# Attention scores from operands stacked to 128 rows, with the row of maxima passed through DRAM

## The reference

```python
def block(args):
    qn, qr = args
    s = (jnp.einsum('bqhd,bkhd->bhqk', qn, k_nope)
         + jnp.einsum('bqhd,bkd->bhqk', qr, k_rope)).astype(jnp.float32) * scale
    p = jax.nn.softmax(s, axis=-1).astype(v.dtype)
    return jnp.einsum('bhqk,bkhd->bqhd', p, v)
```

## Time and profile before

| | us |
|---|---|
| median of three runs | 3884.38 (3883.72 to 3888.82) |
| profiled execution, its own time | 3887.53 |
| its span, first to last instruction | 3885.8 |
| TensorE busy | 3559.1 (92%) |
| VectorE busy | 2205.4 (57%) |
| ScalarE busy | 1532.3 (39%) |
| GpSimd busy | 218.2 (6%) |

### The profile page before, as it was taken

How to read it: one execution, slowest core, us unless ns; L and a number is a source line. 1 busy time by engine, 2 the same in 40 slices (tenths; PEclk the granted TensorE clock), 3 DMA queues, 4 the chain that set the end, 5 groups by cost and what they waited for, 6 DMA issues and landing times. The chain is left out here.

```text
span 3885.8 us, 51505 instructions
## 1 busy us (share of the span) xinstructions
PE 3559.1 (92%) x19453; PEld 2991.9 (77%) x19453; DVE 2205.4 (57%) x3803; ACT 1532.3 (39%) x1959; POOL 218.2 (6%) x132
## 2 busy tenths in 40 slices
PE   5999969997999999999599739999999999999991
PEld 4888868875777777776477628999999999999991
DVE  4444457766777777776355454555555555545545
ACT  2111134444666666666223213433333333333335
POOL 0000000001000000000011100100000000000100
PEclk9999989998999999999899859999999999999995
DMA  2112145656211222200433124555555555555546
GB/s 105 60 59 74 53 156 202 217 212 140 53 20 39 55 53 53 53 8 5 144 135 135 76 87 142 162 168 169 158 176 157 157 172 163 167 167 157 165 127 241
DMA packets 314712, 470.46 MB, mean 121 GB/s; under 512 B 79073, under 2 KB 215009, under 8 KB 311905
## 3 DMA queue, kind: packets, MB, share of 16 engines
q1 hardware_dynamic: 302816, 426.94, 34.8%
q0 software_dynamic: 11776, 41.95, 5.1%
HBM read 352.83 MB, written 116.00 MB: 121 GB/s over the span
## 5 line engine op out<-in xcount | busy, mean ns | idle before, releaser
L63 PE MATMUL psum<-xeT_hi,w_hi 128*128 128x320 f32 x2048 | 635.2, 310 | 0.0
L64 PE MATMUL psum<-xeT_lo,w_hi 128*128 128x320 f32 x2048 | 633.5, 309 | 0.0
L65 PE MATMUL psum<-xeT_hi,w_lo 128*128 128x320 f32 x2048 | 633.5, 309 | 0.0
L1915 ACT ACTIVATE w_hi<-w_raw 128x2048 fp32r<-128x2048 f32 x192 | 358.6, 1908 | 295.5 <-PE psum L65 199.5
L1993 DVE TENSOR_TENSOR w_lo<-w_raw,w_hi 128x2048 fp32r<-128x2048 f32 x192 | 432.3, 2285 | 40.3 <-ACT w_hi L1915 40.3
L1228 ACT ACTIVATE p_hi<-psum 128x1024 fp32r<-128x1024 f32 x272 | 279.1, 1026 | 360.6 <-PE psum L65 360.6
L1275 DVE TENSOR_REDUCE mx<-psum 128x1 f32<-128x1024 f32 x256 | 312.9, 1224 | 168.9 <-PE psum L1152 168.9
L63 PEld LDWEIGHTS psum<-xeT_hi,w_hi 128*128 128x128 f32 x2048 | 385.1, 188 | 1.0
L64 PEld LDWEIGHTS psum<-xeT_lo,w_hi 128*128 128x128 f32 x2048 | 385.2, 188 | 0.6
L65 PEld LDWEIGHTS psum<-xeT_hi,w_lo 128*128 128x128 f32 x2048 | 385.2, 188 | 0.0
L1293 DVE TENSOR_TENSOR p_lo<-p_raw,p_hi 128x1024 fp32r<-128x1024 f32 x272 | 333.2, 1225 | 82.8 <-ACT p_raw L1230 79.5
(11 more groups left out here) (323 smaller groups left out, 6835.2 us busy)
## 6 DMA issues: line engine op xcount, KB each, us to landing
w_raw<-in_w_gate SPq DMA_DIRECT2D x64, 1024.0 KB, 6.2
w_raw<-in_w_up SPq DMA_DIRECT2D x64, 1024.0 KB, 9.4
w_raw<-in_w_down SPq DMA_DIRECT2D x64, 1024.0 KB, 5.2
rec<-rec SPq DMA_DIRECT2D x20, 768.0 KB, 3.6
recb<-rec SPq DMA_DIRECT2D x20, 768.0 KB, 5.1
xa<-in_x SPq DMA_DIRECT2D x20, 512.0 KB, 4.4
xb<-in_x SPq DMA_DIRECT2D x20, 512.0 KB, 6.0
xo<-in_x SPq DMA_DIRECT2D x20, 512.0 KB, 3.4
```

What stands on the lines that cost most here:

```text
L63: pe.matmul(out, a[0], b[0], start=first, stop=False)
L64: pe.matmul(out, a[0], b[1], start=False, stop=False)
L65: return pe.matmul(out, a[1], b[0], start=False, stop=last)
L1915: a.activation(w_hi[n % 4][:], raw[n % 4][:], ACT.Copy).then_inc(s["hi_made"], 1)
```

## The change

A score is k_hi q_hi + k_lo q_hi + k_hi q_lo over 96 features, less the maximum. The 288 rows of that sum are laid anew, as 128 + 128 + 32, with the maximum as a 33rd row of the last part:

- `k_a`, `q_a`: nope high by nope high (64), rotary high by rotary high (32), rotary high (keys) by rotary low (queries) (32).
- `k_b`, `q_b`: nope low (keys) by high (64), nope high (keys) by low (64).
- `k_c`, `q_c`: rotary low (keys) by rotary high (32) and the maxima (keys' row -1, queries' row the maximum). The first key tile of a slot has these on partitions 0 to 32, the second on 64 to 96, so `k_c` has half as many columns, and `q_c` holds its rows twice.

A slot's scores are four matmuls of 128 rows and then two of 33 rows. A head's load is then ten transfers of q and k rows (512 rows of 10 KB instead of 320) and two of the values. The first two heads' load have 64 more rows, and `load(0)` has `k_c`, 64 rows of 5 KB in pieces of 512 bytes.

`unit` takes every fourth query instead of 128 in a row, so that `mx4` in row-major order is the row of 512 maxima. `turn_row` and `take_row` are gone. SP stores `mx4` to DRAM (`max_row`, 2 KB), waits for it, and loads it into two partitions of `q_c`; the block's first score waits for both. SP's list is ordered by slots: the row of a block in its `row_slot`, the load of head h + 1 in slot 2 of head h, the output in its `out_slot`. Bank 7 has one user left.

```diff
-        qT = [(sb(f"qT_hi{b}", [P, T], F32R), sb(f"qT_lo{b}", [P, T], F32R)) for b in range(2)]
-        kT = [(latents[0][:, b, :], latents[1][:, b, :]) for b in range(2)]
+        q_a, q_b, q_c = ([sb(f"q_{n}{b}", [P, T], F32R) for b in range(2)] for n in "abc")
+        k_a, k_b = [latents[0][:, b, :] for b in range(2)], [latents[1][:, b, :] for b in range(2)]
+        k_c = latents[2][:, 0:T // 2]
...
+                    def take(dst, src, arrived):
+                        sp.dma_start(dst.bitcast(F32), src).then_inc(arrived[b], 16)
+                    take(k_a[b][0:MN, :], d["kn"][hi, rows, :], hi_in)
+                    take(q_a[b][0:MN, :], d["qn"][hi, rows, :], hi_in)
+                    take(q_a[b][MN:KQ, :], d["qr"][hi, rot, :], hi_in)
+                    if h < 2:
+                        take(k_a[b][MN:KQ, :], d["kr"][hi], hi_in)
+                        take(k_a[b][KQ:P, :], d["kr"][hi], lo_in)
+                    take(q_a[b][KQ:P, :], d["qr"][lo, rot, :], lo_in)
+                    take(k_b[b][0:MN, :], d["kn"][lo, rows, :], lo_in)
+                    take(k_b[b][MN:P, :], d["kn"][hi, rows, :], lo_in)
+                    take(q_b[b][0:MN, :], d["qn"][hi, rows, :], lo_in)
+                    take(q_b[b][MN:P, :], d["qn"][lo, rows, :], lo_in)
+                    for z in range(2):
+                        take(q_c[b][MN * z:MN * z + KR, :], d["qr"][hi, rot, :], lo_in)
...
+                def load_row(n):
+                    g0, h, qb = starts[n]
+                    sp.wait_ge(s["mx4_made"], n + 1)
+                    sp.dma_start(d["max_row"][n % 2].rearrange("(p q) -> p q", q=4), mx4[n % 2][:].bitcast(F32)
+                                 ).then_inc(row_out[n % 2], 16)
+                    sp.wait_ge(row_out[n % 2], 16 * (n // 2 + 1))
+                    for z in range(2):
+                        dst = q_c[h % 2][MN * z + KR:MN * z + KR + 1, 512 * qb:512 * (qb + 1)].bitcast(F32)
+                        sp.dma_start(dst, d["max_row"][n % 2].unsqueeze(0)).then_inc(row_in[n % 2], 16)
...
                 load(0)
                 load(1)
-                for n, (g0, h, qb) in enumerate(starts):
-                    if qb == 0 and 1 <= h < MH - 1:
+                for g in range(-AHEAD, TOTAL + 1):
+                    if g in row_slot:
+                        load_row(row_slot[g])
+                    if g >= SLOTS and g % SLOTS == 2 and g // SLOTS < MH - 1:
+                        h = g // SLOTS
                         sp.wait_ge(s["scored"], h * SLOTS)
                         sp.wait_ge(s["mixed"], h * SLOTS)
                         load(h + 1)
-                    sp.wait_ge(s["o_made"], n + 1)
...
+                    if g in out_slot:
+                        store_out(out_slot[g])
...
                         if qb < 4:
-                            qt, kb = 4 * qb + r // 2, 2 * (r % 2) + z
+                            q, kb = r // 2, 2 * (r % 2) + z
...
-                        ins = pe.matmul(ps[:, unit_bank(n) + z, :], qT[b][0][0:KQ, qt * P:(qt + 1) * P],
-                                        kT[b][0][0:KQ, kb * 512:(kb + 1) * 512], start=True, stop=True)
+                        fourth = slice(512 * qb + q, 512 * (qb + 1), 4)
+                        ins = pe.matmul(ps[:, unit_bank(n) + z, :], q_a[b][0:KQ, fourth],
+                                        k_a[b][0:KQ, kb * 512:(kb + 1) * 512], start=True, stop=True)
...
-                        pe.wait_ge(s["row_made"], block_no(g) + 1)
+                        n = block_no(g)
+                        pe.wait_ge(row_in[n % 2], 32 * (n // 2 + 1))
...
-                        ins = mm3(pe, ps[:, 2 * (g % 2) + z, :], (kT[b][0][0:KQ + 1, rows], kT[b][1][0:KQ + 1, rows]),
-                                  (qT[b][0][0:KQ + 1, q_cols], qT[b][1][0:KQ + 1, q_cols]), True, True)
+                        out = ps[:, 2 * (g % 2) + z, :]
+                        pe.matmul(out, k_a[b][:, rows], q_a[b][:, q_cols], start=True, stop=False)
+                        pe.matmul(out, k_b[b][:, rows], q_b[b][:, q_cols], start=False, stop=False)
+                    t2 = key_tile(j) // 2
+                    for z in range(2):
+                        part = slice(MN * z, MN * z + KR + 1)
+                        ins = pe.matmul(ps[:, 2 * (g % 2) + z, :], k_c[part, t2 * P:(t2 + 1) * P], q_c[b][part, q_cols],
+                                        start=False, stop=True)
```

More of the change, by code:

```diff
@@ L1057, in attention_phase @@
     TOTAL = MH * SLOTS
+    d["max_row"] = nc.dram_tensor("max_row", (2, 512), F32, kind="Internal").ap()
     starts = [(h * SLOTS + 8 * qb, h, qb) for h in range(MH) for qb in range(NB)]
@@ L1069, in attention_phase @@
         mx, den = sb("mx", [P, 8]), sb("den", [P, 4])
-        mx4 = [sb(f"mx4_{b}", [P, 4]) for b in range(2)]
+        mx4 = [sb(f"mx4_{b}", [P, 4], F32R) for b in range(2)]
         hi_in = [c.sem(f"m_hi_in{b}") for b in range(2)]
@@ L1074, in attention_phase @@
         o_out = [c.sem(f"m_o_out{b}") for b in range(2)]
-        names = ("constant_rows scored hi_made raw_made lo_made mixed unit_scored unit_reduced mx4_made row_turned row_made "
+        names = ("constant_rows scored hi_made raw_made lo_made mixed unit_scored unit_reduced mx4_made "
                  "oT_made out_turned den_made o_made").split()
         s = {n: c.sem("m_" + n) for n in names}
+        row_out = [c.sem(f"m_row_out{b}") for b in range(2)]
+        row_in = [c.sem(f"m_row_in{b}") for b in range(2)]
         NBH = NB * MH
@@ L1085, in attention_phase @@
         out_slot = {g0 + (8 if qb < 4 else 2): n for n, (g0, h, qb) in enumerate(starts)}
[L1086 to L1098, removed]
         def unit_bank(n):
@@ L1108, in load @@
                     b = h % 2
[L1109 to L1115, removed]
+                    rows, rot = slice(MN * h, MN * (h + 1)), slice(KR * h, KR * (h + 1))
+                    hi, lo = 0, 1
+                    def take(dst, src, arrived):
[13 more added lines that the diff above has]
+                        take(q_c[b][MN * z:MN * z + KR, :], d["qr"][hi, rot, :], lo_in)
+                    if h == 0:
+                        for z in range(2):
+                            every_second = d["kr"][lo].rearrange("r (t z p) -> z r t p", z=2, p=P)[z]
+                            take(k_c[MN * z:MN * z + KR, :].rearrange("r (t p) -> r t p", p=P), every_second, lo_in)
                     for w in range(2):
@@ L1118, in load, with store_out @@
                                      ).then_inc(v_in[b], 16)
+                def load_row(n):
[7 more added lines that the diff above has]
+                        sp.dma_start(dst, d["max_row"][n % 2].unsqueeze(0)).then_inc(row_in[n % 2], 16)
+                def store_out(n):
+                    g0, h, qb = starts[n]
+                    sp.wait_ge(s["o_made"], n + 1)
+                    sp.dma_start(d["o"][4 * qb:4 * qb + 4, :, h, :].rearrange("t p e -> p t e"), o[n % 2][:]
+                                 ).then_inc(o_out[n % 2], 16)
                 load(0)
                 load(1)
-                for n, (g0, h, qb) in enumerate(starts):
-                    if qb == 0 and 1 <= h < MH - 1:
+                for g in range(-AHEAD, TOTAL + 1):
[3 more added lines that the diff above has]
+                        h = g // SLOTS
                         sp.wait_ge(s["scored"], h * SLOTS)
@@ L1127, in _, with hi_arrivals, lo_arrivals @@
                         load(h + 1)
-                    sp.wait_ge(s["o_made"], n + 1)
-                    sp.dma_start(d["o"][4 * qb:4 * qb + 4, :, h, :].rearrange("t p e -> p t e"), o[n % 2][:]
-                                 ).then_inc(o_out[n % 2], 16)
+                    if g in out_slot:
+                        store_out(out_slot[g])
                 for b in range(2):
                     sp.wait_ge(o_out[b], 16 * NBH // 2)
-            def arrivals(h):
+            def hi_arrivals(h):
                 return 64 + (h // 2) * 48
+            def lo_arrivals(h):
+                return 16 * (8 + (2 if h % 2 == 0 else 0)) + (h // 2) * 16 * 7
             @block.tensor
@@ L1144, in unit @@
                     if j == 0:
-                        pe.wait_ge(hi_in[b], arrivals(h))
+                        pe.wait_ge(hi_in[b], hi_arrivals(h))
                     wait_from_one(pe, s["unit_reduced"], n if n >= 8 else n - 2)
@@ L1148, in unit @@
                         if qb < 4:
-                            qt, kb = 4 * qb + r // 2, 2 * (r % 2) + z
+                            q, kb = r // 2, 2 * (r % 2) + z
                         else:
-                            qt, kb = NTP + 2 * r + z, 4
-                        ins = pe.matmul(ps[:, unit_bank(n) + z, :], qT[b][0][0:KQ, qt * P:(qt + 1) * P],
-                                        kT[b][0][0:KQ, kb * 512:(kb + 1) * 512], start=True, stop=True)
+                            q, kb = 2 * r + z, 4
+                        fourth = slice(512 * qb + q, 512 * (qb + 1), 4)
```

(22 more changed lines are left out.)

2 lines of the change are left out of this document (removed).

## The result

| | before | after |
|---|---|---|
| median of four runs, us | 3886.09 | 4111.55 (4110.85 to 4112.68) |
| span of the profiled execution | 3885.8 | 4110.3 |
| mean granted clock of TensorE | 0.958 | 0.937 |

The change makes the kernel slower: after over before is 1.058, 95% interval 1.0562 to 1.0599. The forecast was 4092 us (3965 to 4165).

What follows compares the result with a forecast made beforehand. The prediction took TensorE's instruction time to bound the attention. Its terms, -45 + 54 + 131 + 19.5 + 48 = +208, on the profiled 3887.5 us gave 4095, less 3.1: 4092 us, range 3965 to 4165.

Steps and rivals of the forecast that it cites:

- row turning off TensorE: Turning the maxima on TensorE, once in each of 40 blocks, goes: 1.12 us each, -44.8 us.
- slots: Score products of the 272 attention slots, four full and two 33-row instead of six: +0.20 us each, +54 us.
- six waits at head loads: TensorE waits for block 1's maxima row behind the next head's bulk load, h = 1 to 6: 21.8 us each, +131.
- clock behind them: After each of six long TensorE waits, half of 6.49 us is lost to the slow clock: 3.25 us each, +19.5.
- start, to the first score: Both first heads load before SP comes to any row, so the first score comes at 960.1, not 911.7: +48.4 us.
- clock at the start: Slow TensorE clock from the first scores on: already paid in the kernel before, so nothing added.
- The switch: Switching TensorE's array to halves and back in each slot: 0.32 us for two switches, from the expert stage's 64-row transposes.
- R1: Rival for the slots: the 33-row pair overlaps with no switch cost, -63 for +54, 3975 us; chance 0.14.
- R2: Rival for the slots: halves run one after the other, both loads bare, +0.43 a slot, 4155 us; chance 0.12.
- The step of the maxima loads: Maxima products' weight loads stepping over three of four elements: taken as 0, bounds 0 to +0.11 a slot (+30 us).
- R3: Rival: the row's DRAM trips pass through the bulk load, so neither start nor block 1 waits: 3893 or 3863 us; chance 0.06.
- R4: Rival: the maxima products' stepped weight load is four times as long, +141 us, 4233 us; chance 0.05.

Runs made afterwards that it cites:

- the fast kernel: The kernel before with only the maxima row by DRAM, every fourth query in the maxima products and loads spread over SP's list, scores still 97 rows: 3848.2 us.
- control: The kernel before with nothing changed but its own loads spread over SP's list: 3888.7 us, 1.0001 of before.
- the spread kernel: The changed kernel with each head's load cut into twelve transfers spread over SP's list, apart from the maxima row: 3934.9 us, 1.0119 of before.

## Why the prediction was right

The direction and the mechanism held, and four of five terms came within 15 us. In us, over the whole kernel:

| step | predicted | measured | from |
|---|---|---|---|
| row turning off TensorE | -45 | -41 | the fast kernel against its control, 3848.2 - 3888.7 |
| slots | +54 (0.20 each) | +79 (0.29 each) | 3.54 against 3.25 |
| six waits at head loads | +131 (21.8 each) | +116 (19.3 each) | 162.4 - 46.7 |
| clock behind them | +19.5 | +19 | the five slots behind each wait, 20.6 to 21.9 us, against 17.9 to 18.0 for the same slots of the spread kernel |
| start, to the first score | +48 | +49 | 960.67 - 911.71, 1.7 of it a later begin of the phase |
| clock at the start | 0 | +4 | 14.56 us at 0.50 instead of 6.49, half of the difference |
| sum | +208 | +226 | the medians differ by 225 |

- *Row turning.* With the row never late, the fast kernel is 3848 where 3846 stood, worked out from 1.12 us a block. The window for the row was as thought: it is late in no quiet block. The first to the last exponential take 41.6 us less than in the control, 1.04 a block where 1.12 was forecast.
- *The six waits.* The store landed with the end of the bulk, as assumed. Counted from the load's second issue, the bulk ended at 32.6 us (33.4 forecast), the two loads took 1.8 us and not 2.8, and TensorE came to the wait at 15.3 (14.5): together the 2.5 us by which each wait was shorter. Rival R3, a row that passes the bulk, failed even with a queue of its own.
- *Start and clock.* The first score came as forecast. Behind the waits the clock was 0.50 for 5.8 to 8.9 us and not for 6.5 each, but that cost 18.9 of 42.6 us, a little less than half, and the two differences cancel. "The cold clock was paid there before too" put the start's clock at nothing more; the slow stretch there was in fact 8 us longer than before.
- *The switch.* Idle in front of the loads was 101.7 and 65.7 us over the slots, 0.37 and 0.25 each, as the 64-row transposes of the expert stage had it. R1 (no cost of a switch) and R2 (halves one after the other) are both refuted: without the switch a slot is 3.23, with both products in one half 3.76. Of the rule in the Trainium skill (TensorEngine Tiling (Array Packing), Key Properties) both halves agree with the trace: the tiles run together, 0.22 us saved, and around the change of mode the weight loads stand idle, as a drain of the engine would have it.
- *The step of the maxima loads* is the term that was mis-sized: "I take 0, nearest to all loads shown", within bounds of 0 to +30 us. It is +34 (3934.9 - 3900.6), 0.13 a slot, and so just outside them. The text had it right where such a load would show: the first one behind the pair, bare. It had the wrong value, because the rows shown were all of contiguous loads and so were not near it. The note on cachelines of the Trainium skill (SBUF — State Buffer) was the better guide. The traces give the stepped load a size, 0.33 us (L1180, median of 544) against 0.19; no run tried another step, so that the lines are the reason is not shown. R4, four times as long, was far too much, though its sign, "a maxima load of over 0.3 us", came: the text took 0.11 us for a load, which is by how much it lengthened a product, and a contiguous load lasts 0.19 already.

With the step at its measured price the slots come to +0.20 + 0.13 = 0.33, a little over the 0.29 seen, so the switch was priced some 0.04 too high. That the total came within 20 us (4092 for 4112) is in part luck: the waits were priced 15 us too high and the slots 25 too low.

## What to carry to other kernels

A small transfer on which the critical engine waits should not share a time with bulk transfers: of the 177 us that this cost here, a queue of its own gave back 78, and cutting the bulk into pieces between the small ones all. Halving TensorE's array for one pair of products did not pay: it saved 0.46 us of products and spent 0.52. Whether more products per change of mode would pay, no run shows. Before a change is judged as a whole, price its parts alone: here one part was worth 1% and was buried under the other.

## What the runs showed of the hardware

- Two 33-row products in opposite halves overlap nearly fully: 0.50 us for the two, against 0.73 in one half.
- A change between full and half rows keeps a weight load from being begun early on both sides: 0.37 us idle going in, 0.25 coming out, in nearly every slot.
- A weight load of 128 columns stepping over three of four 4-byte elements lasted 0.33 us against 0.19 for a contiguous one; beside products it cost nothing that shows (a slot of the old scores is 3.25 us with either).
- 2 KB from 128 partitions to DRAM, from issue to landing: 2.1 us in 16-byte pieces (median of the changed kernel; 1.4 with the loads spread), 8.3 in 4-byte pieces, 5.5 behind bulk transfers on SP's queue, and up to 10.0 beside them on GpSimd's own.
- The issue of one 640 KB transfer behind others held SP's list for 21.26 us.
- After six waits of about 19 us the granted clock stayed at 0.50 for 5.8 to 8.9 us, and after 46.7 us for 14.56.
